# Delta layer of a hybrid decoder step: chunk work in stacked 64x64 blocks for eight heads, inverse levels of one tile beside the state work of the tile before

## What is computed

```python
G = jnp.cumsum(g, axis=-1)
dec = jnp.exp(jnp.where(tri, G[..., :, None] - G[..., None, :], -jnp.inf))
kb = k * beta[..., None]
A = jnp.where(stri, jnp.einsum('bhncd,bhnsd->bhncs', kb, k) * dec, 0.0)
Tm = lax.linalg.triangular_solve(eye + A, ..., left_side=True, lower=True)
u = jnp.einsum('bhncs,bhnse->bhnce', Tm, v * beta[..., None])
w = jnp.einsum('bhncs,bhnsd->bhncd', Tm, kb * jnp.exp(G)[..., None])
attn = jnp.einsum('bhncd,bhnsd->bhncs', q, k) * dec
...
def step(S, xs):
    v_new = u_i - jnp.einsum('bhcd,bhde->bhce', w_i, S)
    o_i = jnp.einsum('bhcd,bhde->bhce', qe_i, S) + jnp.einsum('bhcs,bhse->bhce', attn_i, v_new)
    S = S * dl_i[..., None, None] + jnp.einsum('bhcd,bhce->bhde', kd_i, v_new)
    return S, o_i
```

## Time and profile before

| | |
|---|---|
| median of 3 runs | 3235.45 us (3234.66 to 3239.74) |
| profiled execution | 3235.7 us |
| its span | 3233.9 us |
| mean granted clock of PE | 0.94 |
| PE busy | 3020.6 us, 93% |
| DVE, ACT, POOL busy | 1464.2, 948.8, 644.7 us |

### The profile page before, as it was taken

The page is one execution under the profiler, slowest core; times in us unless marked ns, Lnnn a source line. Parts: engine busy times, 40 slices in busy tenths (PEclk is TensorE's granted clock), DMA queues, the critical chain, the costliest instruction groups (busy, mean ns, idle before and its releaser), DMA issues.

```text
span 3233.9 us, 53195 instructions
## 1 busy us (share of the span) xinstructions
PE 3020.6 (93%) x23019; PEld 2875.0 (89%) x23019; DVE 1464.2 (45%) x2066; ACT 948.8 (29%) x1679; POOL 644.7 (20%) x544
## 2 busy tenths in 40 slices
PE   7998799999999888898999993999999998899998
PEld 7996599999999888878999993999999984899998
DVE  4552343334675444444433347443355542444332
ACT  5554222222334211112222221222225543322222
POOL 0001141123210222203311142321140002322213
PEclk9998799999999988877999996999999998999999
DMA  3236334343323000032334330434342246233342
GB/s 106 74 89 188 107 93 128 126 130 115 98 74 82 1 1 1 1 95 63 108 121 129 124 119 24 125 121 125 125 129 64 78 127 201 61 119 120 125 128 98
DMA packets 440928, 318.67 MB, mean 99 GB/s; under 512 B 17181, under 2 KB 427214, under 8 KB 438359
## 3 DMA queue, kind: packets, MB, share of 16 engines
q1 hardware_dynamic: 430967, 277.52, 28.5%
q0 software_dynamic: 9728, 37.75, 3.7%
HBM read 299.94 MB, written 71.68 MB: 115 GB/s over the span
## 4 chain that ended last, share of the span: by engine, by line
PE 84%; DVE 8%; ACT 3%; issue 2%; DMA 2%; SPq 1%; POOL 0%; ACTq 0%; DVEq 0%
PE acc L208 65%; PE acc L937 2%; PE misc L1597 1%; PE misc L924 1%; PE misc L881 1%; PE misc L1505 1%; PE acc L1601 1%; PE acc L1630 1%; PE acc L1629 1%; PE misc L1589 1%; DMA s_kv<-cache_a_kv 1%; PE acc L1632 1%; ACT a_sw L1061 1%; PE misc L827 1%; ACT a_p L1017 1%
## 5 line engine op out<-in xcount | busy, mean ns | idle before, releaser
L208 PE MATMUL acc<-act_hi,w_hi 128*128 128x272 f32 x3856 | 818.4, 294 | 21.5 <-DVE act_lo L258 13.0
L208 PE MATMUL acc<-act_lo,w_hi 128*128 128x272 f32 x3856 | 803.3, 290 | 0.0
L208 PE MATMUL acc<-act_hi,w_lo 128*128 128x272 f32 x3856 | 803.1, 290 | 0.0
L193 DVE TENSOR_TENSOR w_lo<-w_raw,w_hi 128x1024 fp32r<-128x1024 f32 (+1 forms) x367 | 582.9, 1588 | 315.9 <-ACT w_hi L186 314.5
L208 PEld LDWEIGHTS acc<-act_hi,w_hi 128*128 128x128 f32 x3856 | 609.3, 190 | 29.0 <-issue 14.5
L208 PEld LDWEIGHTS acc<-act_lo,w_hi 128*128 128x128 f32 x3856 | 610.8, 190 | 0.0
L208 PEld LDWEIGHTS acc<-act_hi,w_lo 128*128 128x128 f32 x3856 | 610.1, 190 | 0.0
L186 ACT ACTIVATE w_hi<-w_raw 128x1024 fp32r<-128x1024 f32 (+1 forms) x367 | 387.9, 1057 | 742.6 <-PE acc L208 685.7
L208 PE MATMUL acc<-h_hi,w_hi 128*128 128x272 f32 x2048 | 425.6, 289 | 0.0
L208 PE MATMUL acc<-h_lo,w_hi 128*128 128x272 f32 x2048 | 422.4, 287 | 0.0
L208 PE MATMUL acc<-h_hi,w_lo 128*128 128x272 f32 x2048 | 422.0, 287 | 0.0
(11 more groups left out here) (357 smaller groups left out, 2934.7 us busy)
## 6 DMA issues: line engine op xcount, KB each, us to landing
w_raw<-mlp_w SPq DMA_DIRECT2D x256, 512.0 KB, 4.0
new_a_kv_s<-cache_a_kv SPq DMA_DIRECT2D x128, 381.0 KB, 4.6
s_kv<-cache_a_kv POOLq DMA_DIRECT2D x40, 768.0 KB, 6.4
w_raw<-a_w_in SPq DMA_DIRECT2D x54, 512.0 KB, 4.2
w_raw<-b_w_in SPq DMA_DIRECT2D x32, 512.0 KB, 4.1
w_raw<-a_w_out SPq DMA_DIRECT2D x16, 576.0 KB, 4.4
s_kv<-cache_a_kv POOLq DMA_DIRECT2D x32, 192.0 KB, 4.0
new_a_kv_s<-cache_a_kv SPq DMA_DIRECT2D x16, 372.0 KB, 4.6
```

What stands on the lines that cost most here:

```text
L193: nc.vector.tensor_tensor(w_lo[:, t.slot, 0:t.kt, :], w_raw[:, t.raw, 0:t.kt, :], w_hi[:, t.slot, 0:t.kt, :].bitcast(F32), ALU.subtract).t ...
L208: last = nc.tensor.matmul(acc[:, t.first % 2, s, 0:HALF], w[:, t.slot, k, :], a[:, k, s * HALF:(s + 1) * HALF], start=(k == 0 and i == 0), ...
```

## The change

Only the chunk work of layer 1 and what touches its buffers changes; the source's other lines move by two or more line numbers.

- Pair data (`e1`, `e2`, `M`, `T`, `U`, `Z`) is no longer a 128x128 matrix per head, but two 64x64 blocks stacked on the partitions: chunk 0 on 0-63, chunk 1 on 64-127, 64 columns per head, all eight heads in one 512-column operation. The matmuls of the levels are done per head and chunk with 64 rows and 64 columns, on partitions 0-63 into 0-63 and 64-127 into 64-127, alternating (`rows_of`).
- The two halves of the heads are no longer worked in turn: one bank per product (`misc[0]`, `misc[1]`, `misc[2]`), one operation each on ACT, DVE and POOL.
- The state work of tile i-1 stands between the levels 0 to 2 of tile i, and the preparation of tile i+1 between the levels 2 to 5, on every engine's queue. Buffers that two tiles now hold at once are doubled (`kt`, `vt`, `kd`, `eg`, `e1`, `e2`); -w and v_new lie in the idle `w_raw`.
- The decay differences come from one 512-column matmul into `misc[3]` (`turn_k`), the exponent rows of `eg` still from eight (`decays`). `Z` of level 0 is not copied; DVE reads it from the bank. The factors of w and u are put on `U` after the levels (`scaled`) instead of on k and v before them. In `values`, u is formed with 64 contracted rows and w·S with 128, where both had 128.
- SP loads the sample states after the last products and stores the prompt's state behind them.

```diff
-            for name in ("e1", "e2", "eg", "kbe", "kd", "vb", "T", "U", "Z"):
-                work[f"b_{name}"] = place.enter_context(nc.sbuf_tensor(f"b_{name}", [P, 2, 4, P], F32))
+            for name in ("kt", "vt", "kd", "eg"):
+                work[f"b_{name}"] = place.enter_context(nc.sbuf_tensor(f"b_{name}", [P, 2, 8, P], F32))
+            for name in ("T", "U", "Z"):
+                work[f"b_{name}"] = place.enter_context(nc.sbuf_tensor(f"b_{name}", [P, 8, 64], F32))
...
+        b_wn, b_V = w_raw[:, 0, 0:HB_, :], w_raw[:, 1, 0:HB_, :]
...
+                    nc.tensor.matmul(misc[3][0:w, :], b_tri[0:w, 1 if i < QT else 3, 0:w], b_gt[0:w, :, :].rearrange("p h n -> p (h n)"),
+                                     start=True, stop=True).then_inc(b_gp, 1)
+                    for h in range(HB_):
+                        last = nc.tensor.transpose(both(0, w)[:, h, :], b_qkv[:, HB_ + h, tc], ident[:, :])
+                    last.then_inc(b_kvT, 1)
...
+                def products(i):
+                    o = i * P
+                    pe.wait_ge(b_kvc, 2 * i + 1)
+                    for bank, first in ((0, HB_), (1, 0)):
+                        for h in range(HB_):
+                            for r in rows_of(i):
+                                tc = slice(o + r.start, o + r.stop)
+                                last = nc.tensor.matmul(acc[r, 0, bank, h * CHUNK:h * CHUNK + span(i)], b_qkv[:, HB_ + h, tc],
+                                                        b_qkv[:, first + h, tc], start=True, stop=True)
...
+                def above(i, k):
+                    wd = span(i)
+                    pe.wait_ge(b_m, lev(i, k) + 1)
+                    if lev(i, k) >= 1:
+                        pe.wait_ge(b_tu, lev(i, k))
+                    for h in range(HB_):
+                        for r in rows_of(i):
+                            last = nc.tensor.matmul(misc[0][r, h * CHUNK:h * CHUNK + wd], b_M[r, k % 2, h, 0:wd],
+                                                    ident[r, r] if k == 0 else b_U[r, h, 0:wd], start=True, stop=True)
+                    last.then_inc(b_zp, 1)
+
+                def below(i, k):
+                    wd = span(i)
+                    pe.wait_ge(b_zc, dif(i, k) + 1)
+                    if k == 1 and i >= 1:
+                        pe.wait_ge(b_wc, i)
+                    for h in range(HB_):
+                        for r in rows_of(i):
+                            last = nc.tensor.matmul(misc[1][r, h * CHUNK:h * CHUNK + wd], b_T[r, h, 0:wd], b_Z[r, h, 0:wd], start=True, stop=True)
+                    if k < levels_of(i) - 1:
+                        for h in range(HB_):
+                            for r in rows_of(i):
+                                last = nc.tensor.matmul(misc[2][r, h * CHUNK:h * CHUNK + wd], b_Z[r, h, 0:wd], b_T[r, h, 0:wd],
+                                                        start=True, stop=True)
+                    last.then_inc(b_delta, 1)
...
+                def old_weights(i):
+                    wd = span(i)
+                    pe.wait_ge(b_u, i + 1)
+                    for h in range(HB_):
+                        for n, r in enumerate(rows_of(i)):
+                            last = nc.tensor.matmul(misc[1 + n][:, h * CHUNK:h * CHUNK + wd], b_kt[r, i % 2, h, :], b_gt[r, h, 0:wd], start=True, stop=True)
+                    last.then_inc(b_wT, 1)
...
+                def values(i, n):
+                    r = rows_of(i)[n]
+                    pe.wait_ge(b_wc, i + 1)
+                    for hb in range(2):
+                        c = 4 * i + 2 * n + hb
+                        if c >= 2:
+                            pe.wait_ge(b_s, c - 1)
+                        for h in range(4 * hb, 4 * hb + 4):
+                            out = both(0, P)[r, h, :]
+                            nc.tensor.matmul(out, b_Uv[r, h, :], b_vt[r, i % 2, h, :], start=True, stop=False)
+                            last = nc.tensor.matmul(out, b_wn[:, h, r], b_S[:, h, :], start=False, stop=True)
+                        last.then_inc(b_vn, 1)
...
+                def outputs(i, n):
+                    r = rows_of(i)[n]
+                    pe.wait_ge(b_vnc, 4 * i + 2 * n + 2)
+                    pe.wait_ge(b_kv, i + 1)
+                    if 2 * i + n >= 1:
+                        pe.wait_ge(b_oc, 2 * i + n)
+                    for hb in range(2):
+                        for h in range(4 * hb, 4 * hb + 4):
+                            out = misc[3][:, h * CHUNK:(h + 1) * CHUNK]
+                            nc.tensor.matmul(out, b_S[:, h, :], b_eg[:, i % 2, h, r], start=True, stop=False)
+                            nc.tensor.matmul(out, b_V[r, h, :], b_e2[r, i % 2, h, :], start=False, stop=True)
+                        for h in range(4 * hb, 4 * hb + 4):
+                            last = nc.tensor.matmul(both(1, P)[:, h, :], b_kd[r, i % 2, h, :], b_V[r, h, :], start=True, stop=True)
+                        last.then_inc(b_ob, 1)
+
...
-                        for hb in range(2):
-                            pe.wait_ge(b_m, lev(i, k, hb) + 1)
-                            if k == 0:
-                                pe.wait_ge(b_att, 2 * i + hb + 1)
-                            else:
-                                pe.wait_ge(b_tu, lev(i, k - 1, hb) + 1)
-                            for h in range(4):
-                                last = nc.tensor.matmul(misc[2 * hb][0:w, h * P:h * P + w], b_M[0:w, hb, k % 2, h, 0:w],
-                                                        ident[0:w, 0:w] if k == 0 else b_w["U"][0:w, hb, h, 0:w], start=True, stop=True)
-                            last.then_inc(b_zp, 1)
...
+                        above(i, k)
+                        if i >= 1 and k == 0:
+                            values(i - 1, 0)
+                        elif i >= 1 and k == 1:
+                            outputs(i - 1, 0)
+                        elif i >= 1 and k == 2:
+                            outputs(i - 1, 1)
+                        elif k == 3:
+                            turn_v(i + 1)
+                        elif k == 4:
+                            decays(i + 1)
+                        if k >= 1:
+                            below(i, k)
+                        if i >= 1 and k == 1:
+                            values(i - 1, 1)
+                        elif k == 2:
+                            turn_k(i + 1)
+                        elif k == 3:
+                            products(i + 1)
+                    old_weights(i)
+                outputs(QT - 1, 1)
 
...
+                copy_k(0)
+                copy_v(0)
+                exp_pairs(0)
+                exp_tokens(0)
                 for i in range(QT + 1):
+                    if i >= 1:
+                        copy_V(i - 1, 0)
+                    copy_Z(i, 1)
+                    if i >= 1:
+                        copy_o(i - 1, 0)
+                        copy_V(i - 1, 1)
                     if i < QT:
+                        copy_Z(i, 2)
+                        if i >= 1:
+                            copy_o(i - 1, 1)
+                        copy_k(i + 1)
+                        copy_Z(i, 3)
+                        exp_pairs(i + 1)
+                        copy_v(i + 1)
+                        copy_Z(i, 4)
+                        exp_tokens(i + 1)
+                        copy_Z(i, 5)
+                    copy_w(i)
+                copy_o(QT - 1, 1)
...
+                    chain(dve, nc.vector.tensor_tensor(e1, by_head(misc[3][0:w, :])[:, :, 0:wd], per(b_G, i, wd), ALU.subtract))
+                    nc.vector.tensor_tensor(e2, e1, spread(b_pack[:, 1 if i < QT else 2, :], i), ALU.add)
+                    nc.vector.tensor_scalar(e1, e1, 0.0, None, ALU.max).then_inc(b_e, 1)
...
+                def first_level(i):
+                    w, wd = width(i), span(i)
+                    eye = spread(b_pack[:, 3, :], i)
+                    dve.wait_ge(b_zp, lev(i, 0) + 1)
+                    nc.vector.tensor_tensor(b_U[0:w, :, 0:wd], eye, by_head(misc[0][0:w, :])[:, :, 0:wd], ALU.subtract)
+                    nc.vector.tensor_tensor(b_T[0:w, :, 0:wd], eye, b_M[0:w, 0, :, 0:wd], ALU.subtract).then_inc(b_tu, 1)
+
+                def level(i, k):
+                    w, wd = width(i), span(i)
+                    U, T = b_U[0:w, :, 0:wd], b_T[0:w, :, 0:wd]
+                    dve.wait_ge(b_delta, dif(i, k) + 1)
+                    last = nc.vector.tensor_tensor(U, U, by_head(misc[1][0:w, :])[:, :, 0:wd], ALU.subtract)
+                    if k < levels_of(i) - 1:
+                        last = nc.vector.tensor_tensor(T, T, by_head(misc[2][0:w, :])[:, :, 0:wd], ALU.subtract)
+                    last.then_inc(b_tu, 1)
+
...
+                def scaled(i):
+                    w, wd = width(i), span(i)
+                    U = b_U[0:w, :, 0:wd]
+                    dve.wait_ge(b_tu, lev(i, levels_of(i) - 1) + 1)
+                    if i < QT:
```

(27 more changed lines are left out.)

384 lines of the change are left out of this document (186 added, 198 removed).

## The result

The changed kernel takes **3224.55 us** (median of 7 runs, 3220.44 to 3230.23) against 3235.45 us before (7 runs, 3233.58 to 3243.66): ratio 0.996, 95% interval 0.9947 to 0.9972. It is faster, by 11 us. The forecast was 44 us, to 3192; the time lies inside the range, between the forecast and rival B (3240). The profiled execution took 3220.44 us.

A forecast was written before the change was run, and what follows sets the result against it. PE, busy 93% of the span, was taken as the bound. Preparation 10, tile 0 42, three tiles of 70, sample tile 38 and end 2 make 302 us against 346, 44 off: 3192 us, range 3150 to 3255.

The forecast's parts named there:

- rival B: Levels of the inverse: opposite corners do not overlap in one PSUM bank, 0.12 us a matmul, 3240 us; chance 0.18.
- the price of the new instructions: PE work per full tile at full clock: 64x64 matmuls 0.06 us each, values 0.36; sum 49.2 for 57.8 us.
- E: Levels: every corner costs a change, some 48 us a tile on top, 3370 us or worse; chance 0.05.
- the waits: PE's waits per full tile, mostly in late levels and ahead of w: 6.3 us, before 10.
- what the form misses: Full tile: 2 us added because the clock formula gave 78 of 82 us for the kernel before.
- the bound of 3: Sign for the waits: none over 3 us inside a tile, the largest ahead of w.
- c = 0.45: Full tiles: share of PE's time at the half clock level, 0.34 before; gives 61.7 us of PE, tile 70.
- the forecast's own form: Chunk work: PE's time is full-clock work W/(1 - 0.45c), a half-level matmul taking about 1.8 times as long.
- the 2 for the end: End of chunk work: DVE's last state update and the own-columns copies stand bare, 2 us.
- the alternation over 23 of 49 us: State work: 0.36 us row-changing matmuls, in which the clock fell before, cover 23 of 49 us instead of 12 of 58.
- C: Chunk work: clock stays at the half level nearly throughout, c = 0.85, tile 88 us, 3265 us; chance 0.14.
- D: Chunk work: the clock holds, c = 0.2, tile 61 us, 3155 us, sign a mean clock of 0.9; chance 0.13.

The follow-up runs named there:

- e2_corners_in_turn: Changed kernel with all eight heads of one 64x64 corner queued before those of the other, instead of alternating corners: 3333.51 us.
- e8_outputs_filled: Changed kernel, values and outputs grouped, five idle matmuls per tile in its end waits, one more behind each four heads of outputs: 3143.89 us.
- e4_tail_filled: Changed kernel with five idle 512-column matmuls per tile in the waits at the tile's end: 3187.53 us.
- e3_grouped: Changed kernel with values and outputs reordered in fours, so array rows change less often: 3171.61 us.
- e7_grouped_filled: Changed kernel with values and outputs grouped in fours and five idle matmuls per tile in its end waits: 3152.19 us.
- e9_fill_elsewhere: Changed kernel with five idle matmuls per tile in a dense place, behind the products of level 3: 3241.96 us.
- e11_before_grouped: Kernel before the change with only its outputs grouped by fours: 3211.73 us.

## Why the prediction failed

**Right: the price of the new instructions.** The mask products take 1.08 us for 32 records at the full clock (1148.11 to 1149.19), 0.034 a record for the forecast 0.03; corners overlap in one bank, on different partitions. The Trainium skill, page "TensorEngine Tiling (Array Packing)", section Restrictions and Gotchas, has it that different row tiles can't access the same PSUM bank at once. These corners do overlap in one bank, and the measurement decides. B's tile of 83.5 at a clock of 0.83 did not come. B's price of 0.12 a matmul is nearly that of another order of the same matmuls (0.11 in e2_corners_in_turn). E falls with B. Values cost 0.36 each as forecast, where a row change is 0.145. The sum of them was a little short: the work of a tile is 52 us at the full clock, not 49: tile 1 of e8_outputs_filled is 54.45 of PE, less nine idle matmuls of 1.05, plus 48 row changes of 0.145.

**Nearly right: the waits.** 76.70 less 71.35 is 5.35 in a tile; I had 6.3 and 2 for what the form misses, 3 too many. The largest is the one ahead of w, 3.2 us, a little over the bound of 3 that I had set.

**Wrong: c = 0.45, the share of PE's time at the half level.** Mean clocks of 0.70, 0.68 and 0.65 are c = 0.60, 0.64 and 0.70; in the sample tile, for which I had put 38 us on 30 of work (c of some 0.45 too), it was 1. With c = 0.62 the forecast's own form gives 49.2/0.72 = 68 us of PE instead of 61.7; with the 52 of work, 72, and 71.35 was measured. For the sample tile 30 us at 1.8 is 54, with the 2 for the end 56, and 56.2 was measured. So in tile 1 PE took 9.7 us more than forecast: 3.5 for the work of 52 (52/0.80 is 65), 6 for the clock; the waits came out 3 lower. That the extra work and the shorter waits nearly cancel is luck. What is left, some 6 us or more in each of tiles 1 to 3 and 16 in the sample tile, is the clock, and as large as the miss.

What failed in the reasoning: I took c as an average to be shifted a little, and did not ask in what state each stretch *starts*. In the kernel before, the last levels are dense and the state work behind them begins at full speed; the clock falls only in its course. In the changed kernel the levels are short, their waits at the tile's end lie close together, and the state work comes right behind them. It then begins at half speed and stays there for 28 us on end; after 10 us at full speed the outputs lose the clock again, for 13. I named both ingredients (the alternation over 23 of 49 us, the waits close together) and counted them as a shift from 0.34 to 0.45. Filling the waits takes the start at half speed away (e4_tail_filled, tile 67.8), grouping shortens the stretch at half speed (e3_grouped, 63.4), and only both together with idle matmuls in the outputs (e8_outputs_filled) give a clock of 1.00.

**Rivals.** By the number alone the kernel stands at the lower edge of B's 3225 to 3255; B's mechanism isn't there, so that is chance. C was nearest in mechanism: the clock stays low. Its c of 0.85 was too much because the clock does come back twice in tile 1, in the differences of level 1 at 1142 and with the next tile's first matmul (L1586), behind those of level 2, at 1165, as I had held against it in part. Its sample tile of 50 was closer than mine, and still short. D, the clock holds, didn't come: no tile of the changed kernel has the 0.9 that was to show it. e7_grouped_filled comes to it (0.88 and 0.91) and e8_outputs_filled passes it (1.00, a tile of 55.4).

**Open.** Why grouping either half also raised the clock of tile 3; what in the outputs loses the clock; and at which point of the tail it falls, which differs between tiles of one execution with the same instructions and waits.

## What to carry to other kernels

Here the change made short the levels, in most of which the kernel before has its full clock. Before counting the gain of such a change, walk through the new order and note at each boundary which level of the clock the next stretch starts with, then price each stretch at that level. Try dense work, even idle work, where waits cluster ahead of work that doesn't bring the clock back; in a dense place it only cost here. And look at the order inside accumulating pairs first: here 48 changes between 64 and 128 rows per tile were worth 57 us, and nearly half as much (26) lay open in the kernel before.

## What the runs showed of the hardware

- Opposite 64x64 corners of the array overlap when they alternate in the queue, also into the same PSUM bank on different partitions: 1.15 us for 32 records at the full clock (after), 1.90 when the eight heads of one corner go before those of the other (e2_corners_in_turn).
- A matmul whose contracted rows change from 64 to 128 or back costs 0.145 us more at the full clock and 0.19 at the half one (values of e3_grouped against the changed kernel).
- TensorE can work without a gap and be kept at the half level: 28 us at 0.50 in the changed kernel. The clock can also fall without any wait, in outputs that change rows at each matmul (at 1152 there) and in grouped ones (at 1131 in e3_grouped).
- A waiting TensorE can make the kernel faster by being given more to do: five idle matmuls of about 1 us in a tile's waits took 9 us off a tile and 41 off the kernel (e4_tail_filled); in a dense place they added 15 (e9_fill_elsewhere).
- In the grouped runs only the first matmul of a group on a PSUM bank has start=True; with start=False on the others their products land as fresh values, in columns of their own, so that the halves of several accumulating pairs can be grouped (e3_grouped, e11_before_grouped).
